# A hybrid decoder step on one core: the MLPs' down-projections by Strassen's scheme

## The chip, the cores and the metric

The program runs on one core of a Trainium2 chip. The metric is the device time of one execution in microseconds. The engines are TensorE (PE in the profile, its weight loads PEld), VectorE (DVE), ScalarE (ACT), GpSimd (POOL) and SyncE (SP), which only issues DMAs. They run side by side and wait for each other by semaphores.

## The reference

One inference step of a decoder with two trunk layers, for a prompt of 1024 tokens and 64 sample tokens, which share all weights: 1088 token columns. Layer 0 mixes by sparse and windowed attention, layer 1 by a gated linear recurrence. Each is followed by the MLP that the change is about:

```python
D_MODEL = 1024
D_FF = 4 * D_MODEL
def sq_relu_mlp(xn, w1, w2):
    h = jax.nn.relu(jnp.einsum('btd,df->btf', xn, w1))
    return jnp.einsum('btf,fd->btd', h * h, w2)
```

All is float32. `xn` is the RMS-normed x, and the result is added to x.

## The kernel before

**Layout.** Activations lie transposed: a tile has 128 features on the partitions and the 1088 columns in three chunks of 364, 364 and 360 (padded to 1092). `d.x` has the 8 tiles of x, `d.gh` and `d.gl` the high and low part of x times its gain. Every float32 product is made of three TensorE products of rounded values (fp32r): high x high, low weight x high, high weight x low (`Dense.product`, L2254 to 2269). So weights and activations are split: the high part is a rounded copy, the low part the difference.

**Weights** come in units of 128 x 1024 (512 KB), one per up tile (8 contraction tiles for one hidden tile) or, in the down-projection, one for two output tiles with four contraction tiles each. SP loads them into one of two slots of `unit_raw` (L2238 to 2241), DVE rounds (`split_high`, L2243 to 2246), POOL subtracts (`split_low`, L2248 to 2251). Both are done for unit u+2 while PE works on u+1, once u is free.

**MLP** (`stage_mlp`, from L2515). The 32 hidden tiles are worked in 8 blocks of `NF` = 4. `up(b)` makes 4 hidden tiles of 72 matmuls each. For each, ACT takes it from PSUM with a relu (L2617), DVE multiplies by the norm's reciprocal root (L2667), ACT squares into the rounded high part (L2619), DVE squares in float32 (L2672), POOL subtracts for the low part (L2593). `down(b)` makes a partial sum of 8 output tiles from these 4, 36 matmuls each, and DVE adds each to x (L2680). The first pair of output tiles takes the fourth hidden tile last (L2652 and on). Two PSUM tiles of three banks (`d_ps`) alternate in the up and the down part; `d_ps_sums` has the two banks between them, for sums of squares. The blocks 0 to 6 are a loop with register values in the waits, the last is written out.

**Around it.** At the end of the first MLP's last block, each finished tile of x is split for the next stage (`part_high` on ACT L2284, `part_low` on DVE L2289), squared (ACT, L2296), and POOL adds up the squares (`sum_up`, L2305). A stage begins with `opening`: its first two products and the matmuls that sum the squares over the partitions. The order of all this is that of the program text, engine by engine.

## Time and profile before

| | |
|---|---|
| median of 3 runs | 2729.66 us (2729.09 to 2733.43) |
| span of the profiled execution | 2722.7 us, 7.0 us less than the median |
| PE busy | 2632.0 us, 97% |
| DVE busy | 1141.8 us, 42% |
| POOL busy | 957.9 us, 35% |
| ACT busy | 781.5 us, 29% |
| attention and projections, until PE's chain of L2263 begins | 784 us |
| first MLP with its opening | 784 to 1617 us, about |
| recurrent stage | 1617 to 1945 us, about |
| second MLP | 1945 to 2719 us, about |

The page has the profiled execution's span and no other time of it; what lies around the span is taken as the 7.0 us to the median. A busy PE is not PE at its peak: the ends of matmuls are modelled and overlap, so the pace of the matmuls is read from their starts. A group's mean is the time of one instruction from start to end. L2263 is the line of nearly all dense matmuls, L2250 and L2246 those of all weight splits, so groups are told apart by the tiles' names.

### The profile page before, as it was taken

To read this page: it belongs to the slowest core of one execution; us is meant where nothing else is said; L and a number is where in the kernel's file an instruction comes from. 1 tells how busy PE (TensorE), PEld (TensorE's weight loads), DVE (VectorE), ACT (ScalarE), POOL (GpSimd) and SP (SyncE) were. 2 spreads that over 40 slices of the span, in tenths; PEclk is the share of its full clock that TensorE was granted. 3 is DMA by queue.
4 is the path that set the end of the run, shared out by engine and by line. 5 is a ranking of instruction groups with operands and counts; after the bars stand their busy time and mean duration, and the time that the engine had idled before them with its cause. 6 is when DMAs were issued, how large, how long until landed. Compare 5 with 4: busy or idle time off the path is not lost.

```text
span 2722.7 us, 39752 instructions
## 1 busy us (share of the span) xinstructions
PE 2632.0 (97%) x15960; PEld 2445.2 (90%) x15960; DVE 1141.8 (42%) x1978; ACT 781.5 (29%) x1400; POOL 957.9 (35%) x470
## 2 busy tenths in 40 slices
PE   7999999989889999999999999999999999999999
PEld 6667787857579999999999999988999999999999
DVE  5369875446555222222222266563532222222222
ACT  5357883866422001001001133452201001100100
POOL 4114440037245234234234362334334234333332
PEclk9999999989889999999999999999999999999999
DMA  4412223642641111111111111232111111111112
GB/s 145 135 26 80 84 89 105 205 113 76 193 178 50 44 46 40 45 46 46 39 46 44 41 54 57 96 130 101 41 47 41 44 46 39 46 45 39 46 43 85
DMA packets 109197, 198.65 MB, mean 73 GB/s; under 512 B 22710, under 2 KB 62774, under 8 KB 108806
## 3 DMA queue, kind: packets, MB, share of 16 engines
q1 hardware_dynamic: 104602, 191.85, 22.3%
q10 hardware_dynamic: 4480, 5.27, 0.6%
q8 instruction: 72, 1.18, 0.2%
q14 instruction: 43, 0.34, 0.0%
HBM read 170.97 MB, written 47.17 MB: 80 GB/s over the span
## 4 chain that ended last, share of the span: by engine, by line
PE 65%; issue 3%; POOL 2%; ACT 1%; DVE 1%; DMA 0%; POOLq 0%; DVEq 0%; ACTq 0%
PE d_ps L2263 63%; POOL m_hidden_low L2593 2%; PE d_ps L2886 1%; POOL unit_low L2250 1%; ACT m_relu L2617 1%; PE d_ps L2278 1%; DVE unit_high L2246 0%; PE d_ps_sums L2321 0%; POOL r_conv_in L2799 0%; DMA mixed_low<-mixed_t 0%; DVE mixed_low L2463 0%; POOL r_input_gate L2793 0%; POOLq L2539 0%; DVE xg_low L3014 0%; DVE x_t L2680 0%
## 5 line engine op out<-in xcount | busy, mean ns | idle before, releaser
L2250 POOL TENSOR_TENSOR unit_low<-unit_raw,unit_high 128x1024 fp32r<-128x1024 f32 x160 | 454.2, 2839 | 1192.0 <-DVE unit_high L2246 1191.3
L2263 PE MATMUL d_ps<-xg_high,unit_high 128*128 128x364 f32 (+1 forms) x2112 | 472.5, 332 | 6.9 <-DVE xg_low L3014 4.3
L2263 PE MATMUL d_ps<-xg_low,unit_high 128*128 128x364 f32 (+1 forms) x2112 | 465.1, 328 | 0.0
L2263 PE MATMUL d_ps<-xg_high,unit_low 128*128 128x364 f32 (+1 forms) x2112 | 465.0, 328 | 0.0
L2617 ACT ACTIVATE m_relu<-d_ps 128x1092 f32<-128x1092 f32 x64 | 69.2, 1082 | 1177.8 <-PE d_ps L2263 1177.8
L2680 DVE TENSOR_TENSOR x_t<-x_t,d_ps 128x1092 f32<-128x1092 f32 x128 | 165.3, 1292 | 520.1 <-PE d_ps L2263 520.1
L2263 PEld LDWEIGHTS d_ps<-xg_high,unit_high 128*128 128x128 f32 x2112 | 366.7, 189 | 11.8 <-DVE xg_low L3014 4.6
L2263 PEld LDWEIGHTS d_ps<-xg_high,unit_low 128*128 128x128 f32 x2112 | 367.2, 189 | 0.0
L2263 PEld LDWEIGHTS d_ps<-xg_low,unit_high 128*128 128x128 f32 x2112 | 365.7, 189 | 0.0
L2263 PE MATMUL d_ps<-m_hidden_high,unit_high 128*128 128x364 f32 (+1 forms) x1536 | 340.6, 330 | 3.8 <-POOL m_hidden_low L2593 3.8
L2263 PE MATMUL d_ps<-m_hidden_high,unit_low 128*128 128x364 f32 (+1 forms) x1536 | 338.5, 328 | 0.0
L2263 PE MATMUL d_ps<-m_hidden_low,unit_high 128*128 128x364 f32 (+1 forms) x1536 | 337.7, 328 | 0.0
L2667 DVE TENSOR_TENSOR m_relu<-m_relu,rstd_all 128x1092 f32<-128x1092 f32 x64 | 86.4, 1350 | 562.2 <-ACT m_relu L2617 562.2
L2263 PEld LDWEIGHTS d_ps<-m_hidden_high,unit_high 128*128 128x128 f32 x1536 | 264.0, 188 | 11.8 <-POOL m_hidden_low L2593 8.6
L2263 PEld LDWEIGHTS d_ps<-m_hidden_high,unit_low 128*128 128x128 f32 x1536 | 265.8, 188 | 0.0
L2263 PEld LDWEIGHTS d_ps<-m_hidden_low,unit_high 128*128 128x128 f32 x1536 | 265.6, 188 | 0.0
L785 PE MATMUL proj_ps<-w_high,x_high 128*128 128x512 f32 (+2 forms) x520 | 202.8, 390 | 13.7 <-POOL w_low L608 12.7
L785 PE MATMUL proj_ps<-w_low,x_high 128*128 128x512 f32 (+2 forms) x520 | 198.8, 382 | 0.0
L785 PE MATMUL proj_ps<-w_high,x_low 128*128 128x512 f32 (+2 forms) x520 | 198.3, 381 | 0.0
L2593 POOL TENSOR_TENSOR m_hidden_low<-m_square,m_hidden_high 128x1092 fp32r<-128x1092 f32 x64 | 163.4, 2554 | 6.4 <-DVE m_square L2672 6.4
L785 PEld LDWEIGHTS proj_ps<-w_high,x_high 128*128 128x128 f32 x520 | 99.8, 192 | 47.3 <-POOL w_low L608 13.9
L2246 DVE CAST unit_high<-unit_raw 128x1024 fp32r<-128x1024 f32 x158 | 111.8, 707 | 63.2 <-PE d_ps L2263 59.8
(370 smaller groups left out, 3090.0 us busy)
## 6 DMA issues: line engine op xcount, KB each, us to landing
unit_raw<-w_units SPq DMA_DIRECT2D x160, 512.0 KB, 3.6
unit_raw<-w_in SPq DMA_DIRECT2D x48, 256.0 KB, 2.9
proj_rows<-rows SPq DMA_DIRECT2D x32, 256.0 KB, 2.0
s_win<-win_cache SPq DMA_DIRECT2D x2, 3968.0 KB
proj_rows<-rows SPq DMA_DIRECT2D x36, 128.0 KB, 1.8
sw_rows<-proj_rows SPq DMA_DIRECT2D x12, 384.0 KB, 4.8
select_work<-xt SPq DMA_DIRECT2D x8, 546.0 KB, 4.1
x_t<-xt SPq DMA_DIRECT2D x4, 1092.0 KB, 13.6
```

The lines of the kernel that those rows point to most:

```text
L785: last = nc.tensor.matmul(ps[p % 3][:, 0:w], x[:, k, c:c + P], y[gi % 2][:, k, 0:w], start=(n == 0), stop=(n == len(passes) - 1))
L2246: self.nc.vector.tensor_copy(self.wh[slot][:, :], self.raw[:, slot, :]).then_inc(self.w_high, 1)
L2250: self.nc.gpsimd.tensor_tensor(self.wl[slot][:, :], self.raw[:, slot, :], self.wh[slot][:, :].bitcast(F32), ALU.subtract).then_inc(self.w_ ...
L2263: last = self.nc.tensor.matmul(ps[:, c, 0:USED[c]], w[wslot][:, wk], v[:, k, c, 0:USED[c]], start=(k == 0 and n == 0), stop=(k == nk - 1 a ...
L2278: last = self.nc.tensor.matmul(ps[:, c, 0:USED[c]], w[wslot][:, wk], v[:, k, c, 0:USED[c]], start=(k == 0 and n == 0), stop=(k == nk - 1 a ...
L2593: nc.gpsimd.tensor_tensor(hl[:, i, :, :], v[:, i % 2, :, :], hh[:, i, :, :].bitcast(F32), ALU.subtract).then_inc(h_low, 1)
L2617: nc.scalar.activation(r[:, i % 2, :, :], ps[slot][:, :, 0:CH], ACT.Relu).then_inc(d.taken[slot], 1)
L2667: nc.vector.tensor_tensor(r[:, i % 2, :, :], r[:, i % 2, :, :], d.rstd[:, :, :], ALU.mult).then_inc(relu_scaled, 1)
L2680: nc.vector.tensor_tensor(d.x[:, n, :, :], d.x[:, n, :, :], ps[s][:, :, 0:CH], ALU.add).then_inc(d.taken[s], 1)
L2886: last = nc.tensor.matmul(ps[use % 2][:, c, 0:CC], gw[:, n % 2, x, :], cv[:, n % 2, c, :], start=True, stop=True)
```

## The change

Both down-projections are computed by Strassen's scheme in Winograd's form. Take a pair of output tiles, two pairs of hidden tiles and the two halves of the columns (544 each): that is a 2 x 2 matrix of weights (each entry 256 deep) times a 2 x 2 matrix of hidden values, 8 half-size products. The scheme forms four sums of weights (`weigh`, DVE, 256 columns) and four sums of hidden values (`combine`, DVE, 544 columns), takes seven products (`part`), and adds them up in seven steps (`add`, DVE). Products 0 to 3 start four quarters of PSUM, products 4 to 6 go on in quarters 0, 2 and 3. What is common to several outputs gathers over all blocks in `shared_part` (`y2`) and is given out in the last block (`share`). Each product is 2 contraction tiles x 3 kinds x 2 chunks of 272 columns = 12 matmuls, so a block has 4 x 84 = 336 matmuls of 272 columns in its down-projection in place of 288 of 364, 364 and 360.

With it:
- The high parts of the hidden values are now ACT's copies of seven matrices of 544 columns per pair and contraction tile (`hidden_high`), the low parts POOL's (`hidden_low`); DVE takes the up product from PSUM with relu and reciprocal root in one (`spread_hidden`), ACT squares in place.
- A down unit is split in four parts, high by ACT (`high_of_parts`), low by POOL (`low_of_parts`), in place in the one pair of slots: the first half once product 3 of the pair before is done, the second once all seven are.
- Block b now makes the hidden tiles 4b+2 to 4b+5; the last block has two up tiles, and the pair made of them is used at once.
- A stage's opening waits for all adds of the MLP before it, since PSUM is shared.

```diff
+            def hidden_low(pair, q, s):
+                i = SPLIT_ORDER[s]
+                pool.wait_ge(h_high, NPROD * pair + s + 1)
+                nc.gpsimd.tensor_tensor(hl[:, i, q, :], SOURCES[i], hh[:, i, q, :].bitcast(F32), ALU.subtract).then_inc(h_low, 1)
...
+                for m in range(PAIRS):
+                    low_of_parts(PAIRS * b + m, m % 2, (2, 3) if last and m == 0 else range(4))
+                    if last and y is None:
+                        for o in (2 * m, 2 * m + 1):
+                            d.sum_up(pool, [v[:, i, :].rearrange("p (c n) -> p c n", c=NCH) for i in range(2)], o, seen)
+                if not last or y is None:
+                    for k in range(2):
+                        d.split_low(pool, W0 + NF * b + (6 if not last else 4) + k, k)
...
+            def high_of_parts(n, slot, which):
+                for x in which:
+                    act.wait_ge(wsums_made, 4 * n + (2, 3, 4, 4)[x])
+                    src, wide = weight_parts(d.raw[:, slot, :], wsum, x)
+                    nc.scalar.activation(part_slots(d.high, x), src, ACT.Copy).then_inc(part_high, 1)
...
+                for m in range(1, PAIRS):
+                    act.wait_ge(part_made, PART_MADE_0 + NPROD * (n + m - 1) + 4)
+                    high_of_parts(n + m, m % 2, (0, 1))
+                    act.wait_ge(part_made, PART_MADE_0 + NPROD * (n + m))
+                    high_of_parts(n + m, m % 2, (2, 3))
+                    if last and y is None:
+                        next_rows(m - 1)
...
+            def next_rows(m):
+                for o in (2 * m, 2 * m + 1):
+                    act.wait_ge(added, ADDED_0 + NPROD * (PAIRS * LAST + m) + 6 + o % 2)
+                    d.part_high(act, o, layer + 1)
+                    d.square(act, [v[:, i, :].rearrange("p (c n) -> p c n", c=NCH) for i in range(2)], o, seen)
...
+            def part(i, qs):
+                out = d.quarter[BLOCK_OF_PRODUCT[i]]
+                for q in qs:
+                    c0 = 2 * P * (i % 4) + P * q
+                    for x, (w, h) in enumerate(((d.high, hh), (d.low, hh), (d.high, hl))):
+                        for c in range(2):
+                            last = nc.tensor.matmul(out[:, c, :], w[:, i // 4, c0:c0 + P], h[:, i, q, HC * c:HC * (c + 1)],
+                                                    start=(i < 4 and q == 0 and x == 0),
+                                                    stop=(q == 1 and x == 2), skip_group_check=(i >= 4))
+                if qs[-1] == 1:
+                    last.then_inc(part_made, 1)
+
+            def ready(n, i):
+                pe.wait_ge(part_low, PART_LOW_0 + 4 * n + (1, 2, 1, 2, 3, 4, 3)[i])
+                pe.wait_ge(added, ADDED_0 + NPROD * n + (-2, -5, -1, 0, 1, 3, 4)[i])
...
+                        for i in range(4):
+                            if i == 2:
+                                pe.wait_ge(d.taken[1], R0 // 2 + pairs)
+                            ready(n, i)
+                            part(i, (0,))
+                        for i in range(4):
+                            pe.wait_ge(h_low, 2 * NPROD * b + NPROD + SPLIT_ORDER.index(i) + 1)
+                            part(i, (1,))
...
+            def spread_hidden(pair, t, first=False):
+                dve.wait_ge(d.made, R0 + 2 * pair + t + 1)
...
+                nc.vector.scalar_tensor_tensor(out=v[:, t, :].rearrange("p (c n) -> p c n", c=NCH), in0=d.ps[t][:, :, 0:CH], scalar=0.0,
+                                               in1=d.rstd[:, :, :], op0=ALU.max, op1=ALU.mult).then_inc(d.taken[t], 1)
...
+                for m in range(PAIRS):
+                    ahead = (n + m + 1, (m + 1) % 2, load_of(b, k0 + m + 1)) if m < PAIRS - 1 else None
+                    add(n + m, m, 0)
+                    if ahead:
+                        weigh(*ahead, 0)
+                    add(n + m, m, 1)
+                    if last:
+                        share(m)
...
+                    if not last and m == 1:
                         for x in range(2):
...
+                            combine(2 * b + 2, x)
+                    add(n + m, m, 4)
+                    add(n + m, m, 5)
```

**Order, POOL, last block of the first MLP, before.** `unit_low` is the low part of a whole unit, `square_sum` the running sum of the squares of x.

```order
L2250 TENSOR_TENSOR unit_low<-unit_raw,unit_high 128x1024
L2305 TENSOR_TENSOR square_sum<-square_sum,m_square 128x1092 x2
L2250 TENSOR_TENSOR unit_low<-unit_raw,unit_high 128x1024
L2305 TENSOR_TENSOR square_sum<-square_sum,m_square 128x1092 x2
L2250 TENSOR_TENSOR unit_low<-unit_raw,unit_high 128x1024
L2305 TENSOR_TENSOR square_sum<-square_sum,m_square 128x1092 x2
```

The same place after the change. The parts of 2 x 256 and 256 columns are the four lows of one pair of output tiles.

```order
L2655 TENSOR_TENSOR unit_low<-unit_raw,unit_high 128x2x256
L2655 TENSOR_TENSOR unit_low<-m_weight_sums,unit_high 128x2x256
L2655 TENSOR_TENSOR unit_low<-unit_raw,unit_high 128x2x256
L2655 TENSOR_TENSOR unit_low<-m_weight_sums,unit_high 128x256
L2325 TENSOR_TENSOR square_sum<-square_sum,m_hidden 128x1092 x2
L2270 TENSOR_TENSOR unit_low<-unit_raw,unit_high 128x1024 x2
```

Before, the low behind a pair of sums is that of a unit which PE takes one unit later; now all four lows of a pair stand behind the two sums of the pair before, and both units of the next opening behind the last two sums.

**Order, ACT, at the same place, after.** `unit_high` are the high parts of a pair of output tiles, `xg_high` and `m_hidden` the high part and the square of a row tile of x.

```order
L2713 ACTIVATE unit_high<-unit_raw 128x2x256
L2713 ACTIVATE unit_high<-m_weight_sums 128x256
L2304 ACTIVATE xg_high<-x_t,params 128x1092
L2316 ACTIVATE m_hidden<-x_t 128x1092
L2304 ACTIVATE xg_high<-x_t,params 128x1092
L2316 ACTIVATE m_hidden<-x_t 128x1092
```

The squares of a pair's two row tiles stand behind all high parts of the next pair; before, ACT had nothing but rows here.

**Order, DVE, second pair of output tiles in a middle block, after.** The adds read `d_ps`, the others are sums of weights and of hidden values; `square_sum` serves as their buffer.

```order
L2884 TENSOR_TENSOR x_t<-x_t,d_ps 128x544
L2873 REGISTER_ALU
L2874 REGISTER_ALU
L2875 TENSOR_TENSOR m_weight_sums<-unit_raw,m_weight_sums 128x256
L2842 REGISTER_ALU
L2844 REGISTER_ALU
L2845 TENSOR_TENSOR square_sum<-m_hidden 128x544
L2847 REGISTER_ALU
L2848 REGISTER_ALU
L2849 TENSOR_TENSOR m_hidden<-m_hidden 128x544
L2881 REGISTER_ALU
L2884 TENSOR_TENSOR x_t<-x_t,d_ps 128x544
```

Before, DVE had two adds of 128x1092 and one `unit_high` of 128x1024 (L2246) for a pair; now the fourth and the fifth add of a pair have a weight sum and two hidden sums between them.

## Rows read from the trace of the kernel before

**Rows 1.** Chain of waits, middle blocks of the first MLP: start us, us, what
```profile
1080.75 1.09 ACT m_relu L2617
...
1089.83 87.16 PE d_ps L2263 x522
1177.09 1.09 ACT m_relu L2617
```

**Rows 2.** TensorE in order of time at a down-projection's start: start us, us, instructions
```profile
992.08 0.66 PE L2263 MATMUL d_ps<-m_hidden_high,unit_low 128*128 128x364 f32 x3
...
992.58 0.66 PE L2263 MATMUL d_ps<-m_hidden_low,unit_high 128*128 128x364 f32 x3
...
993.49 0.77 PE L2263 MATMUL d_ps<-m_hidden_high,unit_high 128*128 128x364 f32 x3 [0.25 <-POOL m_hidden_low L2593]
```

**Rows 3.** The page's costliest groups: operation, shapes, count | busy us, mean ns | idle before
```profile
L2250 POOL TENSOR_TENSOR unit_low<-unit_raw,unit_high 128x1024 fp32r<-128x1024 f32 x160 | 454.2, 2839 | 1192.0 <-DVE unit_high L2246 1191.3
...
L2680 DVE TENSOR_TENSOR x_t<-x_t,d_ps 128x1092 f32<-128x1092 f32 x128 | 165.3, 1292 | 520.1 <-PE d_ps L2263 520.1
...
L2263 PE MATMUL d_ps<-m_hidden_high,unit_low 128*128 128x364 f32 (+1 forms) x1536 | 338.5, 328 | 0.0
...
L2593 POOL TENSOR_TENSOR m_hidden_low<-m_square,m_hidden_high 128x1092 fp32r<-128x1092 f32 x64 | 163.4, 2554 | 6.4 <-DVE m_square L2672 6.4
```

**Rows 4.** TensorE in order of time, matmuls of 256 columns, first and 26th
```profile
443.07 0.28 PE L785 MATMUL proj_ps<-w_low,x_high 128*128 128x256 f32 x1
...
446.05 0.28 PE L785 MATMUL proj_ps<-w_high,x_low 128*128 128x256 f32 x1
```

**Rows 5.** DVE's groups, shapes kept apart
```profile
L2672 DVE TENSOR_TENSOR m_square<-m_relu 128x1092 f32<-128x1092 f32 x64 | 82.5, 1288 | 0.1
...
L2116 DVE TENSOR_TENSOR ss_merge_shared<-select_work,ss_merge_shares 128x256 f32<-128x256 f32 x15 | 6.0, 453 | 0.0
...
L2956 DVE TENSOR_TENSOR r_conv_in<-d_ps,rstd_all 128x364 f32<-128x364 f32 x8 | 4.2, 524 | 0.0
```

**Rows 6.** ACT's groups, shapes kept apart
```profile
L2619 ACT ACTIVATE m_hidden_high<-m_relu 128x1092 fp32r<-128x1092 f32 x64 | 71.7, 1120 | 93.6 <-DVE m_relu L2667 93.6
...
L2284 ACT ACTIVATE xg_high<-x_t,params 128x1092 fp32r<-128x1092 f32 x24 | 28.6, 1206 | 78.2 <-DVE x_t L2507 47.2 <-DVE x_t L2680 30.4 <-PE d_ps L2263 0.6
...
L741 ACT ACTIVATE rows_sq<-rows 128x512 f32<-128x512 f32 x36 | 22.8, 632 | 3.6 <-ACT rows L721 0.4
```

**Rows 7.** POOL's groups, shapes kept apart
```profile
L608 POOL TENSOR_TENSOR w_low<-unit_raw,w_high 128x512 fp32r<-128x512 f32 x48 | 64.5, 1350 | 99.8 <-DVE w_high L928 99.8
...
L2305 POOL TENSOR_TENSOR square_sum<-square_sum,r_decay 128x1092 f32<-128x1092 f32 x3 | 7.2, 2409 | 0.0
...
L608 POOL TENSOR_TENSOR w_low<-unit_raw,w_high 128x256 fp32r<-128x256 f32 x8 | 6.7, 856 | 13.4 <-DVE w_high L928 13.4
```

**Rows 8.** In order of time, DVE and POOL at once, in two places
```profile
987.34 1.29 DVE L2672 TENSOR_TENSOR m_square<-m_relu 128x1092 f32<-128x1092 f32 x1
987.50 3.39 POOL L2250 TENSOR_TENSOR unit_low<-unit_raw,unit_high 128x1024 fp32r<-128x1024 f32 x1 [6.05 <-DVE unit_high L2246]
...
1612.83 3.46 POOL L2250 TENSOR_TENSOR unit_low<-unit_raw,unit_high 128x1024 fp32r<-128x1024 f32 x1 [2.25 <-DVE unit_high L2246]
1613.93 3.50 DVE L2289 SCALAR_TENSOR_TENSOR xg_low<-x_t,params,xg_high 128x1092 fp32r<-128x1092 f32 x1
```

**Rows 9.** TensorE in order of time behind two idle stretches
```profile
1836.65 3.32 PE L2886 MATMUL d_ps<-r_conv,own_a 128*128 128x371 f32 x6 [3.09 <-DVE square_sum L2979]
...
1852.23 1.28 PE L2263 MATMUL d_ps<-xg_high,unit_high 128*128 128x364 f32 x3 [4.29 <-DVE xg_low L3014]
...
1857.83 0.71 PE L2263 MATMUL d_ps<-xg_high,unit_high 128*128 128x364 f32 x3
```

**Rows 10.** Two stretches: us, each engine's busy us (count), granted clock, DMA share, GB/s
```profile
732.30:739.80 7.50, 6.96 (x138) 3.81 (x141) 4.79 (x23) 2.90 (x13) 2.91 (x4) 1.00 0.40 107
1855.00:1858.00 3.00, 3.00 (x12) 3.00 (x11) 2.97 (x3) 0.00 (x0) 0.00 (x0) 0.51 0.63 275
```

More of the change, by code:

```diff
@@ L2160 @@
 NBLK = FF // (NF * P)
-BLK_U, BLK_R = 2 * NF, NF + KD
+BLK_U = 2 * NF
 U_OUT = 0
@@ L2357, with stage_out_projection @@
 FIRST_KS = 4
-def stage_out_projection(nc, a, d, ident, mixed, own, oth, otl):
+def stage_out_projection(nc, a, d, ident, mixed, own, oth, otl, used):
     with ExitStack() as ctx:
@@ L2384, in stage_out_projection @@
         OWN = 16 * own.LOADS
+        freed = released(nc, used)
         @block.sync
@@ L2395, in _ @@
             for u in range(4, KD + 2):
-                d.load(sp, u, u % 2)
+                d.load(sp, u, u % 2, u)
         @block.gpsimd
         def _(pool):
+            for first, count in runs_of(freed):
+                nc.gpsimd.sem_clear(range(first, first + count))
             nc.gpsimd.memset(d.ones[:, :], 1.0).then_inc(d.ready, 1)
@@ L2558, in _, with run, unit_at, load_of @@
+        def run(eng, body):
+            with eng.Fori(0, LAST) as b:
+                body(b, False)
+            body(LAST, True)
+        def unit_at(b, k):
+            return U0 + 2 + BLK_U * b + k
+        def load_of(b, k):
+            return U0 // 2 + 1 + BLK_U // 2 * b + k // 2
+        def tile_at(b, k):
+            return NF * b + 2 + k
+        def down_at(b, last):
+            return 2 if last else NF
         @block.sync
         def _(sp):
-            def up(b):
-                for i in range(NF):
-                    u, slot = up_at(b, i)[:2]
-                    d.load(sp, u + 2, slot)
@@ L2565, in down, with load, body @@
-            def down(b):
-                for m in range(NF):
-                    u, slot = down_at(b, m)[:2]
-                    if not isinstance(u, int) or u + 2 < U_END:
-                        d.load(sp, u + 2, slot)
-            run(sp, up, down)
+            def load(u, slot):
+                if isinstance(u, int) and u >= U_END:
+                    return
+                d.load_unit(sp, u, slot)
+            def body(b, last):
+                k0 = down_at(b, last)
+                for k in range(k0):
+                    sp.wait_ge(d.w_low, W0 + tile_at(b, k) + 1)
+                    load(unit_at(b, k + 2), k % 2)
+                for m in range(PAIRS):
+                    sp.wait_ge(part_low, PART_LOW_0 + 4 * (PAIRS * b + m) + 4)
+                    load(unit_at(b, k0 + m + 2), m % 2)
@@ L2596, in down @@
[L2596 to L2605 removed]
+            nc.gpsimd.sem_inc(part_made, PART_MADE_0)
@@ L2607, in _ @@
+            pool.wait_ge(d.made, R0 + 1)
+            nc.gpsimd.memset(y2[:, :, :], 0.0).then_inc(cleared, 1)
+            for k in range(2):
+                d.split_low(pool, W0 + k + 2, k)
+            run(pool, body)
         @block.scalar
@@ L2621, in down, with square_hidden @@
-            def down(b):
-                if isinstance(b, int) and y is None:
-                    for n in range(KD):
-                        _, _, _, _, slot, used = down_at(b, n // 2)
-                        act.wait_ge(d.taken[(slot + n) % 2], used + (slot + n % 2) // 2 + 1)
-                        d.part_high(act, n, layer + 1)
-                        d.square(act, [v[:, 0, :, :], v[:, 1, :, :]], n, seen)
-            run(act, up, down)
+            def square_hidden(tile, t):
+                act.wait_ge(d.taken[t], R0 // 2 + tile + 1)
+                nc.scalar.activation(v[:, t, :], v[:, t, :], ACT.Square).then_inc(squared, 1)
@@ new lines, in next_rows @@
+            def next_rows(m):
[3 more added lines that the diff above has]
+                    d.square(act, [v[:, i, :].rearrange("p (c n) -> p c n", c=NCH) for i in range(2)], o, seen)
+            for t in range(2):
+                square_hidden(0, t)
+            act.wait_ge(d.made, R0 + 2)
+            unit_high(W0 + 3, 1, U0 // 2 + 1)
+            run(act, body)
@@ L2656, in _, with up @@
-            run(pe, up, down)
+            d.opening(pe, W0, R0, nth)
+            def up(b, k):
+                t = k % 2
+                pe.wait_ge(d.w_low, W0 + tile_at(b, k) + 1)
+                pe.wait_ge(d.taken[t], R0 // 2 + 2 * b + 1 + k // 2)
+                pe.wait_ge(added, ADDED_0 + NPROD * (PAIRS * b - 1) + (5 if t == 0 else NPROD))
+                d.product(pe, d.ps[t], t, 0, KD, d.gh, d.gl)
+            def part(i, qs):
[9 more added lines that the diff above has]
+                    last.then_inc(part_made, 1)
@@ new lines, in _, with weight_parts @@
+            for t in range(2):
+                spread_hidden(0, t, True)
+            dve.wait_ge(cleared, 1)
+            for x in range(2):
+                combine(0, x, True)
+            run(dve, body)
+        return added, ADDED_0 + NPROD * PAIRS * NBLK
+def weight_parts(raw, wsum, x):
+    if x < 2:
+        src = raw[:, 0:4 * P] if x == 0 else wsum[:, 0:2, :].rearrange("p a n -> p (a n)")
+    else:
+        src = raw[:, 4 * P:8 * P] if x == 2 else wsum[:, 2, :]
+    return (src.rearrange("p (a n) -> p a n", a=2), 2) if x < 3 else (src, 1)
```

389 lines of the change are left out of this document (264 added, 125 removed).

## The prediction

> **What bounds the kernel now.** I read the chain of waits first. In both MLPs it is TensorE, interrupted once per block of four hidden tiles: 87.16 us of L2263, then ACT, DVE and POOL in turn, and again [rows 1]. One block lasts 1177.09 - 1080.75 = 96.34 us and holds 576 matmuls, 288 up and 288 down. The view in order of time shows what the interruption costs: three matmuls start every 0.50 us, but between 992.58 and 993.49 there are 0.91 us, because the down-projection waits for the fourth tile's low part from POOL; with the slow restart it is about 0.6 us [rows 2]. So a matmul of 362.7 columns on average costs (96.34 - 0.6) / 576 = 166.2 ns, and nothing else in the MLPs matters. The costliest groups show how much room the other engines have: POOL's hidden lows, L2593, are 163.4 us in the whole run, its unit lows, L2250, 454.2, DVE's adds, L2680, 165.3 [rows 3].
>
> The profiled span is 2722.7 us; the times shown have a median of 2729.66, so 7.0 us lie around the span. All differences below are put on the span and carried to that median.
>
> **Matmuls.** Down-projections now: 3 x 1536 = 4608 matmuls (one of the three groups, which differ by 1%, stands in [rows 3]); 4608 x 166.2 ns = 765.8 us. After: 16 blocks x 4 pairs of output tiles x 7 products x 12 matmuls = 5376, of 272 columns. No row has 272 columns. Between 443.07 and 446.05, 25 matmuls of 256 columns start, 119.2 ns each [rows 4], also with a weight load for each; between that and 166.2 ns at 362.7 the line gives 126 ns at 272. 5376 x 126 = 677.4 us: **-88.3 us**. Bounds: 119.2 (-125) and 133 ns (-51). I take the line, close to the 256 row. A fixed part of some 7 ns per matmul eats 3 us of the 91.5 us for which the columns alone stand. The Trainium skill (TensorE: Matmul & The Clock Gate, Back-to-back issue gap) has columns / 2.4 plus 2.5 ns, so 153.6 ns before and 115.8 after, and the sum would be -85.3 us; the trace has more time at both sizes.
>
> The old wait goes with the old order: 16 x 0.6 = **-9.6**. In the middle blocks hidden pair 2b+1 is made two up tiles before it is used, 24 us (2 x 72 x 166.2 ns), and its seven highs and lows need 7 x 0.66 on ACT and 7 x 1.36 on POOL (544 columns; between 0.63 for 512 and 1.12 for 1092 on ACT, 1.35 and 2.55 on POOL [rows 3, 6, 7]): hidden. PSUM is now released by DVE, behind the reciprocals of an opening, and no longer by ACT ahead of them; DVE's 1.3 us bound what the first up tile can wait for that (0 to 1.3, twice), I take 0.4: **+0.8**.
>
> **DVE and POOL in the middle blocks.** A pair of output tiles lasts 84 x 126 = 10.6 us on PE. DVE has seven adds (0.71 each, between 0.52 for 364 and 1.29 for 1092 columns) and four weight sums (0.45, as L2116): 6.8 us [rows 3, 5]. POOL has lows of 512, 512, 512 and 256 columns, 1.35 x 3 + 0.86 = 4.9 us [rows 7]. Both fit. But they block each other: L2672, with both inputs in SBUF, beside L2250 makes the latter 3.39 us for 1024 columns, where L2305 has 2.41 for 1092 [rows 7], and L2289, begun 1.1 us into an L2250, lasts 3.50, where L2672 has 1.29 for as many columns [rows 5, 8]. The Trainium skill (SBUF - State Buffer, Who interferes with whom) says it as a lock held for a whole instruction by whichever started first, when the DVE instruction has two SBUF inputs. The trace agrees with its 3.39 and 3.50 us; it speaks against this change, since weight sums, hidden sums and lows are all of that kind.
> It shows at the step from the second pair to the third, where two hidden sums (0.73 each) stand ahead of the fifth add, and the first product of the next pair needs that add. From the end of the fourth product (6.05 us into the pair) DVE does 0.71 + 0.45 + 1.46 + 0.71 and handovers of 0.3: 9.7 of 10.6 us, 0.9 left. POOL's two lows of 1.3 fall in the same stretch. Once in the way they cost 0.4, twice 1.7; which, hangs on whether ACT's high (0.63) or DVE's add (0.71) ends first. I take 1.2 x 14 blocks = **+16.8** (0 to 24).
>
> **The last block of each MLP** has two up tiles, and hidden pair 15 is used at once. From the end of the second: DVE 1.3, ACT square 1.12, DVE sum 0.73, ACT high 0.66, two lows 2.7, handovers 0.4: 6.9 us. PE has four half products and one more, 3.8 us: wait 3.1. Then product 5 needs the low of the third weight part, which on POOL stands behind all seven hidden lows, and the last of these behind DVE's fourth sum: two lows 2.7, sum 0.73, high 0.66, low 1.36, part low 1.3 = 6.8 after 6.9, less what PE does meanwhile (2.3): 4.5, and with DVE's L2892/L2893 (0.73 + 1.29) in POOL's way up to 7.4. I take 6.2. Together 9.3 x 2 = **+18.6** (15 to 21).
>
> **The last block of the first MLP** is the worst place. POOL adds up the squares of rows 2m and 2m+1 before it makes any low of pair m+1 (the order shows it), and these squares are ACT's last work behind the highs of pair m+1, which wait for pair m's last product. So PE ends pair m, and then: highs 0.63 + 0.42, the rows' high and square (L2304, L2316) twice, (1.21 + 1.12) x 2 = 4.7, POOL's sum 2.4 to 2.6, the first low 1.3, handovers 0.3 to 0.6: 9.7, 10.1 and 10.1 us of idle PE, **+29.9** [rows 3, 6, 7]. Before, the next unit's low stood ahead of these sums, one unit early; that cover is gone. The recurrent stage's opening hangs on the same: unit high 1.06, 4.7, sum 2.5, POOL behind one xg_low of DVE 1.3, unit low 2.3, handovers 0.5: **+12.4** (10 to 14). The second MLP has no squares.
>
> **Clock.** After 4.29 us of idle PE, from 1852.23 on, the granted clock was half, 0.51 between 1855 and 1858 [rows 9, 10]. From 1852.23 to 1857.83 PE starts 18 matmuls in 5.60 us, where 18 x 166.2 ns are 3.0: 2.6 us lost. After the 3.09 us at 1836.65 six matmuls of 371 columns take 3.32 us, 0.55 each, and I take less, 2.0. Six new gaps are longer (three between pairs, the opening, one per last block): 6 x 2.3 = **+13.8** (9 to 20). A slow stretch ahead of the second wait of a last block disappears in it.
>
> The end is shorter: the last add 0.71 instead of 1.29, **-0.6**.
>
> Sum: -88.3 - 9.6 + 0.8 + 16.8 + 18.6 + 29.9 + 12.4 + 13.8 - 0.6 = -6.2. On 2729.7 that is 2723.5, so **2724 us**. Of 98.5 us won, 92.3 are spent again, 9.3 + 29.9 + 12.4 + 5 x 2.3 = 63 of them in the first MLP's last block.
>
> **Rivals.**
> *The engines stay out of each other's way.* DVE wins the port: 0.4 us per middle block, 7.5 per last block, gaps of 9 us with 2 us of clock. -6.2 - 11.2 - 3.6 - 4 = -25: 2705. For it: POOL and DVE are busy for 35% and 42% of the span now, by the table. Against: their starts come from the same product's end.
> *DVE becomes the bound in the middle blocks (slower).* Four weight sums per pair, each behind a low of 1.3, are 6.8 + 5.2 = 12.0 against 10.6 us of PE. If half of this comes true, each of the 14 blocks waits 3 us instead of 1.2: +25, 2749. It decides for slower than before once a middle block waits over 1.7 us. For it: nearly every DVE step also has two or three register steps ahead of it. Against: lows fill only 4.9 of 10.6 us.
> *PE's queue or the weight load sets the pace.* A product is 24 instructions and two or three register steps in 1.51 us, 56 ns each; the row of 256 columns shows 59.6 ns and no less. Were that the floor, a product would take 1.61: +0.1 x 392 = +38, 2762. Against: 138 matmuls and 141 loads in 7.5 us at 732.3, 27 ns each, though of smaller tiles [rows 10].
> *The order does not bite* (the squares come early enough, so the gaps of the first MLP's last block are not there): 2724 - 42 - 9 = 2673. The order speaks plainly against it.
>
> **Numbers.** Forecast 0.55, first rival 0.2, second 0.14, third 0.06, fourth 0.05. The forecast's own range is 2712 to 2736. A measurement of this kernel tells 0.2%, 5.5 us, from no change, so faster means below 2724.2: half of the forecast's weight lies there. Faster 0.27 + 0.2 + 0.05 = 0.52, same 0.24, slower 0.04 + 0.14 + 0.06 = 0.24. Range 2700 to 2746.
>
> **What would show it.** Sets of two matmuls of 272 columns 0.25 us apart; middle blocks of 48 + 42.3 + 1.2 = 91.5 us in the chain; in the last block of the first MLP three gaps of about 10 us on PE that end with a POOL low of 512 columns, behind a POOL sum, and one of 12 ahead of the opening; half clock behind each. If the gaps are there but the blocks last 90.5 us, the first rival is right; if PE's sets are 0.27 apart without waits, the third. A total below 2700 means that I misread the order.

## The result and the profile after

| | before | after |
|---|---|---|
| median | 2729.38 us (2727.72 to 2733.43, 4 runs) | 2714.87 us (2708.61 to 2716.01, 4 runs) |
| span of the profiled execution | 2722.7 us | 2714.2 us (its own time 2716.01) |

The ratio is 0.9948 [0.9935, 0.9961]: 14.5 us faster, 9 us below the forecast of 2724 and inside its range. Around the span of after lie 1.8 us, not the 7.0 assumed for before. In all executions that are listed with both, span and time differ by 1.7 to 1.9 us, so the profiled execution of before took about 2724.6 us, some 5 us less than its median. That is why the two profiled executions differ by 8.5 us only and the medians by 14.5.

The page after, engines first (busy us, share, instructions), then groups (operation, shapes, count | busy us, mean ns | idle before):

```profile
PE 2561.0 (94%) x16728; PEld 2370.2 (87%) x16728; DVE 1505.1 (55%) x2510; ACT 1043.2 (38%) x1876; POOL 1201.4 (44%) x824
...
L2785 PE MATMUL d_ps<-m_hidden_high,unit_high 128*128 128x272 f32 x1792 | 379.3, 294 | 53.0 <-POOL unit_low L2655 35.9
...
L2655 POOL TENSOR_TENSOR unit_low<-unit_raw,unit_high 128x512 fp32r<-128x512 f32 x128 | 177.6, 1387 | 392.0 <-ACT unit_high L2713 392.0
L2884 DVE TENSOR_TENSOR x_t<-x_t,d_ps 128x544 f32<-128x544 f32 x320 | 227.3, 718 | 151.6 <-PE d_ps L2785 151.2
L2648 POOL TENSOR_TENSOR m_hidden_low<-m_hidden,m_hidden_high 128x544 fp32r<-128x544 f32 x192 | 272.0, 1439 | 77.5 <-ACT m_hidden_high L2702 77.5
```

The adds and lows have the sizes that were put between the neighbours of [rows 3, 5, 7] (forecast 0.71, 1.35 and 1.36 us). PE has less to do than before and is still the chain's main engine, but 35.9 us of its idle time are now POOL's weight lows.

One middle block in the chain of waits (start us, us, what), where [rows 1] had ACT's relu and 87.16 us of one piece:

```profile
942.88 0.72 DVE x_t L2884
943.60 0.04 issue
943.64 21.37 PE d_ps L2785 x168
965.01 47.84 PE d_ps L2283 x288
1012.86 21.12 PE d_ps L2785 x168
1033.98 0.04 issue
1034.01 0.72 DVE x_t L2884
```

A block lasts 1034.01 - 942.88 = 91.13 us (before 96.34), and 168 matmuls of 272 columns take 21.12 us, 125.7 ns each. It is cut once, ahead of the third pair of output tiles. In order of time, on PE, DVE and POOL:

```profile
942.42 0.41 PE L2785 MATMUL d_ps<-m_hidden_low,unit_high 128*128 128x272 f32 x2
943.64 0.52 PE L2785 MATMUL d_ps<-m_hidden_high,unit_high 128*128 128x272 f32 x2 [0.81 <-DVE x_t L2884]
```

```profile
939.41 1.82 DVE L2845 TENSOR_TENSOR square_sum<-m_hidden 128x544 f32<-128x544 f32 x1
941.26 1.70 DVE L2849 TENSOR_TENSOR m_hidden<-m_hidden 128x544 f32<-128x544 f32 x1
942.88 1.97 DVE L2884 TENSOR_TENSOR x_t<-x_t,d_ps 128x544 f32<-128x544 f32 x3
```

```profile
939.15 1.49 POOL L2655 TENSOR_TENSOR unit_low<-unit_raw,unit_high 128x512 fp32r<-128x512 f32 x1 [4.06 <-ACT unit_high L2713]
940.60 1.77 POOL L2655 TENSOR_TENSOR unit_low<-m_weight_sums,unit_high 128x512 fp32r<-128x512 f32 x1
```

DVE's two hidden sums last 1.82 and 1.70 us, not 0.73, each beside a low of POOL's; the fifth add (the first of L2884 at 942.88) comes late and PE loses 1.0 us (1.10 from start to start, where 0.126 is usual). It is so in all 14 middle blocks.

The last block of the first MLP, the chain from the end of its second pair of output tiles:

```profile
1577.67 0.94 ACT unit_high L2713 x2
1578.61 1.09 ACT xg_high L2304
1579.70 1.01 ACT m_hidden L2316
...
1580.78 2.50 POOL square_sum L2325
...
1583.42 2.48 POOL square_sum L2325
1585.90 1.23 POOL unit_low L2655
1587.13 0.04 issue
1587.17 13.60 PE d_ps L2785 x84
```

This is the forecast's chain, step for step; PE's waits from start to start are 9.36, 9.83, 9.83 us, and 12.11 ahead of the opening. For the opening the chain of waits has 10.62 us of "issue" and names nobody. POOL in order of time shows what it waits for:

```profile
1625.96 6.16 POOL L2325 TENSOR_TENSOR square_sum<-square_sum,m_hidden 128x1092 f32<-128x1092 f32 x2 [12.55 <-ACT m_hidden L2316]
1632.08 4.67 POOL L2270 TENSOR_TENSOR unit_low<-unit_raw,unit_high 128x1024 fp32r<-128x1024 f32 x2
```

The first of the two unit lows ends about where PE goes on, at 1634.52. Behind the waits the granted clock is at its lower level, 1.2 of 2.4 GHz, and 84 matmuls take 13.60 us where two pairs of a middle block have 21.12 for 168. Two of the stretches (us, each engine's busy us, clock, DMA):

```profile
1580.00:1593.00 13.00, 5.83 (x25) 5.83 (x26) 1.06 (x2) 2.80 (x3) 9.36 (x6) 0.50 0.12 33
1604.00:1613.50 9.50, 3.19 (x14) 3.20 (x15) 0.07 (x1) 1.93 (x2) 9.27 (x6) 0.50 0.00 0
```

By stage, from PE's starts in order of time (first matmul of the out-projection; first of the four that sum the squares, in each opening; PE's end), profiled executions, us:

| kernel (median) | ahead of the out-projection | to the first sums | first MLP | recurrent | second MLP |
|---|---|---|---|---|---|
| before (2729.4) | 762.2 | 87.9 | 772.6 | 334.6 | 760.7 |
| after (2714.9) | 771.3 | 87.6 | 789.2 | 331.4 | 729.5 |
| e1 lows first (2684.4) | 769.9 | 88.9 | 756.2 | 334.9 | 729.6 |
| e2 hidden sums late (2698.4) | 766.5 | 88.9 | 783.3 | 331.5 | 720.9 |
| e3 short lows (2697.6) | 766.4 | 88.1 | 782.4 | 331.4 | 720.9 |
| e4 before, small scratch (2729.7) | 765.3 | 88.7 | 772.8 | 335.0 | 761.0 |
| e5 parts early (2718.8) | 769.1 | 88.4 | 790.2 | 334.6 | 729.4 |
| e6 three orders (2667.3) | 766.0 | 88.6 | 750.8 | 333.0 | 721.9 |
| e7 short sums (2682.9) | 766.9 | 89.0 | 753.3 | 334.6 | 729.6 |
| e8 busy waits (2709.9) | 767.2 | 87.9 | 784.5 | 335.0 | 728.6 |
| e9 share behind 4th add (2671.5) | 766.2 | 88.7 | 751.9 | 335.1 | 723.9 |
| e10 share behind 7th add (2662.1) | 766.9 | 88.0 | 747.5 | 335.0 | 718.7 |

So the change makes the second MLP 31.3 us shorter and the first 16.6 longer. The first column is the same work in all kernels: it moves by 9 us over these executions and blurs a comparison of two spans. (The two kernels without the change have its two lowest values, 762.2 and 765.3; that the change costs a little there is not excluded.)

### The profile page after: what moved, and what is told of

The parts are those of the page before. It is cut to its first block, busy times and chain, and to the rows that moved or that the text cites. A ratio compares the mean times of both kernels' runs of the same rounds, so it can differ in the third digit from the quotient of the medians.

```text
span 2714.2 us, 44747 instructions
## 1 busy us (share of the span) xinstructions
PE 2561.0 (94%) x16728; PEld 2370.2 (87%) x16728; DVE 1505.1 (55%) x2510; ACT 1043.2 (38%) x1876; POOL 1201.4 (44%) x824
## 4 chain that ended last, share of the span: by engine, by line
PE 65%; DVE 3%; issue 1%; POOL 1%; ACT 1%; DMA 0%; DVEq 0%; ACTq 0%; POOLq 0%
PE d_ps L2283 39%; PE d_ps L2785 24%; PE d_ps L3164 1%; PE d_ps L2298 1%; DVE x_t L2884 1%; POOL square_sum L2325 0%; DVE square_sum L2845 0%; DVE rstd_all L2370 0%; POOL m_hidden_low L2648 0%; DVE xg_low L3292 0%; POOL unit_low L2655 0%; DVE m_hidden L2837 0%; PE d_ps L2343 0%; DVE unit_high L2266 0%; POOL unit_low L2270 0%
## 5 line engine op out<-in xcount | busy, mean ns | idle before, releaser
L2283 PE MATMUL d_ps<-xg_high,unit_high 128*128 128x364 f32 (+1 forms) x2112 | 472.5, 332 | 18.8 <-issue 11.8
L2785 PE MATMUL d_ps<-m_hidden_high,unit_high 128*128 128x272 f32 x1792 | 379.3, 294 | 53.0 <-POOL unit_low L2655 35.9
L2270 POOL TENSOR_TENSOR unit_low<-unit_raw,unit_high 128x1024 fp32r<-128x1024 f32 x96 | 231.2, 2409 | 405.3 <-DVE unit_high L2266 237.6
L2785 PE MATMUL d_ps<-m_hidden_high,unit_low 128*128 128x272 f32 x1792 | 374.2, 290 | 0.0
L2785 PE MATMUL d_ps<-m_hidden_low,unit_high 128*128 128x272 f32 x1792 | 373.6, 290 | 0.0
L2655 POOL TENSOR_TENSOR unit_low<-unit_raw,unit_high 128x512 fp32r<-128x512 f32 x128 | 177.6, 1387 | 392.0 <-ACT unit_high L2713 392.0
L2884 DVE TENSOR_TENSOR x_t<-x_t,d_ps 128x544 f32<-128x544 f32 x320 | 227.3, 718 | 151.6 <-PE d_ps L2785 151.2
L2648 POOL TENSOR_TENSOR m_hidden_low<-m_hidden,m_hidden_high 128x544 fp32r<-128x544 f32 x192 | 272.0, 1439 | 77.5 <-ACT m_hidden_high L2702 77.5
L2713 ACT ACTIVATE unit_high<-unit_raw 128x512 fp32r<-128x512 f32 x128 | 81.0, 633 | 517.8 <-PE d_ps L2785 381.4
L2702 ACT ACTIVATE m_hidden_high<-m_hidden 128x544 fp32r<-128x544 f32 x192 | 118.9, 651 | 224.6 <-DVE m_hidden L2857 129.3
L2837 DVE SCALAR_TENSOR_TENSOR m_hidden<-d_ps,rstd_all 128x1092 f32<-128x1092 f32 x64 | 82.5, 1291 | 206.7 <-PE d_ps L2283 204.8
```

The lines of the kernel that those rows point to most:

```text
L2270: self.nc.gpsimd.tensor_tensor(self.wl[slot][:, :], self.raw[:, slot, :], self.wh[slot][:, :].bitcast(F32), ALU.subtract).then_inc(self.w_ ...
L2283: last = self.nc.tensor.matmul(ps[:, c, 0:USED[c]], w[wslot][:, wk], v[:, k, c, 0:USED[c]], start=(k == 0 and n == 0), stop=(k == nk - 1 a ...
L2648: nc.gpsimd.tensor_tensor(hl[:, i, q, :], SOURCES[i], hh[:, i, q, :].bitcast(F32), ALU.subtract).then_inc(h_low, 1)
L2655: nc.gpsimd.tensor_tensor(out, src, top.bitcast(F32), ALU.subtract).then_inc(part_low, 1)
L2702: nc.scalar.activation(hh[:, i, q, :], SOURCES[i], ACT.Copy).then_inc(h_high, 1)
L2713: nc.scalar.activation(part_slots(d.high, x), src, ACT.Copy).then_inc(part_high, 1)
```

## The experiments

**Lows ahead of the sums of squares** (POOL, last block; result 2684.4 us (2680.3 to 2687.6), ratio to before 0.9827 [0.9804, 0.9850])

```diff
-                for m in range(PAIRS):
-                    low_of_parts(PAIRS * b + m, m % 2, (2, 3) if last and m == 0 else range(4))
+                low_of_parts(PAIRS * b, 0, (2, 3) if last else range(4))
+                for m in range(PAIRS):
+                    if m < PAIRS - 1:
+                        low_of_parts(PAIRS * b + m + 1, (m + 1) % 2, range(4))
+                    elif not last or y is None:
+                        for k in range(2):
+                            d.split_low(pool, W0 + NF * b + (6 if not last else 4) + k, k)
                     if last and y is None:
                         for o in (2 * m, 2 * m + 1):
                             d.sum_up(...)
```

> The changed kernel with one thing moved on POOL, in the last block only: the four lows of a pair of output tiles, and behind the last pair the two unit lows of the next opening, stand ahead of the sums of squares of the pair before. My theory: the order on POOL alone makes the four waits of 9.36, 9.83, 9.83 and 12.11 us; they go but for about 0.9 us ahead of the opening (the last add), 40 us, and with them four of the half-clock stretches, 9 us: 2715 - 49 = about 2666. Rival: ACT or DVE would be late anyhow (the highs wait for the same product), so that each wait only shrinks to some 4 us: 2715 - 25 = about 2690.

Measured: -30.5 us, the first MLP 33.0 shorter and now 16.4 below that of before. So mending the order gave 33 us, where 40 + 9 were put on it; the median, 2684.4, is nearer to the rival's 2690 than to the 2666 of the theory. The waits of 9 to 12 us are gone, waits of 1.3 to 3.7 us have come in their place, and they end with DVE's adds. Of 40 us there, DVE is busy for 38.7 (columns as above):

```profile
1557.00:1597.00 40.00, 30.39 (x223) 29.49 (x222) 38.70 (x36) 18.52 (x23) 28.43 (x16) 0.96 0.14 40
```

In order of time, DVE and POOL:

```profile
1588.37 0.71 DVE L2886 TENSOR_TENSOR m_shared_part<-m_shared_part,d_ps 128x544 f32<-128x544 f32 x1
...
1590.12 2.70 DVE L2894 TENSOR_TENSOR x_t<-x_t,m_shared_part 128x544 f32<-128x544 f32 x1
1592.74 3.60 DVE L2895 TENSOR_TENSOR x_t<-x_t,m_shared_part 128x1088 f32<-128x1088 f32 x1
```

```profile
1586.90 2.08 POOL L2655 TENSOR_TENSOR unit_low<-unit_raw,unit_high 128x512 fp32r<-128x512 f32 x1 [2.77 <-ACT unit_high L2715]
...
1589.64 5.54 POOL L2325 TENSOR_TENSOR square_sum<-square_sum,m_hidden 128x1092 f32<-128x1092 f32 x2
1595.15 3.43 POOL L2270 TENSOR_TENSOR unit_low<-unit_raw,unit_high 128x1024 fp32r<-128x1024 f32 x1
```

The instruction of 1088 columns takes 3.60 us beside POOL's sums and the low behind them, where the one in the chain of e5 below has 1.29; the add of one input from PSUM has its 0.71 beside a low. Two of DVE's groups in these 40 us, weight sums of 256 columns, and the same sum in e3, where POOL's lows are short:

```profile
L2867 DVE TENSOR_TENSOR m_weight_sums<-unit_raw 128x256 f32<-128x256 f32 x2 | 3.6, 1792 | 0.0
L2870 DVE TENSOR_TENSOR unit_raw<-unit_raw 128x256 f32<-128x256 f32 x2 | 3.1, 1553 | 0.1
...
940.61 0.42 DVE L2867 TENSOR_TENSOR m_weight_sums<-unit_raw 128x256 f32<-128x256 f32 x1
```

At the times that they have elsewhere (adds 0.71, row lows 1.27, shared part 0.72 and 1.29, weight sums 0.42) DVE's instructions there would take some 27 us, an estimate. So some 12 us or more of DVE's busy time there are stretch beside POOL. My theory has the cause of the old waits right, the rival (DVE late anyhow) the size of what is left.

**Hidden sums late** (DVE; 2698.4 us (2696.6 to 2699.1), 0.9881 [0.9861, 0.9901])

```diff
-                    if not last and m == 1:
-                        for x in range(2):
-                            combine(2 * b + 2, x)
                     add(n + m, m, 4)
...
                     add(n + m, m, 6)
+                    if not last and m == 1:
+                        for x in range(2):
+                            combine(2 * b + 2, x)
```

> The changed kernel with the two hidden sums of the second pair of output tiles moved behind that pair's last add, so that they no longer stand ahead of the fifth. My theory: the 1.10 us from start to start at the step from the second to the third pair (0.13 elsewhere) go in all 14 middle blocks, 14 x 1.0 = 14 us: about 2701. Rival: DVE is late by its whole load, and the wait turns up at a later product: about 2715.

Measured: -16.4 us; no wait is left in the middle blocks (no two starts over 0.2 us apart), and the two MLPs are 5.9 and 8.6 us shorter.

**Short lows** (POOL makes the weight lows of the second to fourth pair for 32 of 256 columns in middle blocks; the rest of them is left out; 2697.6 us (2691.9 to 2704.6), 0.9882 [0.9854, 0.9911])

```diff
+                    if few:
+                        out, src, top = (t[..., 0:32] for t in (out, src, top))
```

> The changed kernel, with POOL's lows of the second to fourth pair of output tiles made for 32 of each 256 columns in the middle blocks (that part of the low weights is left out); DVE's and ACT's orders as they are. If the 1.0 us at the step to the third pair is the price of POOL's lows standing in DVE's way, it goes here too: about 2702. If it is DVE's queue alone (two hidden sums ahead of the fifth add), it stays: about 2715.

Measured: -17.3 us, the same waits gone, with DVE's order as it was. The two hidden sums, DVE in order of time:

```profile
935.00 0.85 DVE L2847 TENSOR_TENSOR square_sum<-m_hidden 128x544 f32<-128x544 f32 x1
935.88 0.73 DVE L2851 TENSOR_TENSOR m_hidden<-m_hidden 128x544 f32<-128x544 f32 x1
```

1.82 and 1.70 have become 0.85 and 0.73. The wait needs both: POOL's lows beside the hidden sums, and these ahead of the fifth add. "DVE's queue alone" is refuted.

**Before with the small scratch** (2729.7 us (2728.4 to 2735.2), 1.0003 [0.9993, 1.0013])

```diff
-    nc = bacc.Bacc("TRN2", target_bir_lowering=False, num_devices=1)
+    nc = bacc.Bacc("TRN2", target_bir_lowering=False, num_devices=1, dynamic_dma_scratch_size=1024)
```

> The kernel before, with only the smaller scratch of 1024 for dynamic DMAs that the change also brings. In the profiled execution of after, the part ahead of the first MLP lasts 9 us longer, from the sample stage at 731 us on. If the scratch is why: 2729 + 9 = about 2738. If it is the chance of one execution, or the clock: about 2729.

The scratch does nothing; the 9 us are the spread of one stage from execution to execution (first column of the table).

**Third and fourth part early** (last block of both MLPs; 2718.8 us (2715.4 to 2722.3, 3 runs), 0.9956 [0.9940, 0.9973])

```diff
                     for s in range(2, NPROD):
                         hidden_low(2 * b + 1, 1, s)
+                        if s in (4, 5):
+                            low_of_parts(PAIRS * b, 0, (s - 2,))
```
and `high_of_parts(n, 0, (2, 3))` on ACT behind the fifth hidden high.

> The changed kernel; in the last block of both MLPs ACT and POOL make the third and fourth part (high, low) of the first pair of output tiles between the hidden parts for products 4, 5 and 6, not behind all of them. My theory: the second wait of a last block (3.47 and 4.86 us from start to start) is POOL's order. Now product 4 waits for two lows from the end of the first wait on, 2.8 us against 2.3 us of PE, product 5 for two more, and these waits come to about 2 us in place of 3.3 and 4.7: 4 us less in all, about 2711. Rival: DVE's sums and adds are what is late, and the waits stay.

Refuted: the rival holds. In the second MLP product 4 now waits 1.6 us from start to start and product 5 another 4.2, 5.8 in all where product 4 alone had waited 4.9, and both waits end with an add of DVE's. The chain there:

```profile
2671.12 0.04 DVE x_t L2894
2671.16 1.69 issue
2672.86 1.29 DVE x_t L2895
2674.14 0.02 issue
2674.17 0.43 DVE unit_raw L2870
2674.59 0.64 DVE x_t L2886
```

Product 5 needs the third add, and the giving out of the shared part (L2894, L2895) stands ahead of it.

**All three orders** (2667.3 us (2666.2 to 2667.4), 0.9764 [0.9749, 0.9779])

The edits are the three above: those of lows ahead of the sums (e1), hidden sums late (e2) and parts early (e5).

> All three orders together: lows ahead of the sums of squares, hidden sums behind the second pair's last add, third and fourth part of the last block's first pair early. If the three are independent: 2684.4 (the first alone) - 14 (2698.4 against 2714.9 in the second alone would be 16) - 4 = about 2665. If DVE's load sets the last block of the first MLP once POOL's order is mended, the third gives nothing there: about 2669.

2667.3 lies between the two (2665 and 2669): e1's 30.5 and e2's 16.4 add up to 46.9, measured 47.6. So the two parts made early add nothing that can be told from noise, and the result does not decide between the two expectations.

**Short sums of squares** (e1; POOL adds six of the seven squares of the first MLP's last block over 32 of 364 columns, the rest is left out; 2682.9 us (2680.5 to 2691.1), 0.9833 [0.9815, 0.9850])

```diff
+        out, first, second = (t[:, :, 0:32] if seen == KD and n > 1 else t for t in (self.ssum[:, :, :], first, sq[n % 2]))
```

> The kernel with the lows ahead of the sums of squares (2684.4 us), and six of the seven sums of squares of the first MLP's last block made on POOL over 32 of each 364 columns (the rest of these sums is left out); DVE and ACT do all they did. In that block a pair of output tiles now takes 16 us where PE needs 10.6. If that is DVE and POOL shutting each other out: DVE's instructions with both inputs in SBUF (four weight sums 1.8, the shared part 2.0, two row lows 2.5 us) and POOL's (lows 4.9, sums 4.8) are 16.0 in a row, and without the sums 11.3, so that DVE's own 11.4 are the bound: three pairs x 4.6 = 14 us less, 2684 - 14 = about 2670. If DVE's own load with its waits is the bound, nothing changes: about 2684.

Mostly refuted: 1.5 us in the medians, which is within the noise, 2.9 in the stage, not 14. From the first add of the third pair to that of the fourth it is 12.2 us (1569.67 to 1581.89) where e1 has 15.8 (1572.57 to 1588.37), near the 11.3 that was expected; but the opening then waits 5.6 us for the last add, behind two row lows of DVE stretched to 3.4 and 3.2 us, and its clock falls (72 matmuls in 13.77 us, where 166.5 ns each make 12.0). DVE is busy for 35.7 of 37 us even so:

```profile
1554.00:1591.00 37.00, 31.81 (x248) 31.02 (x246) 35.71 (x39) 19.44 (x24) 22.32 (x16) 1.00 0.15 44
```

**Busy waits** (after, 72 matmuls of 240 columns into free columns of PSUM ahead of the second to fourth pair; 2709.9 us (2707.6 to 2711.6), 0.9920 [0.9906, 0.9934])

```diff
+                    if last and y is None and m:
+                        pe.wait_ge(added, ADDED_0 + NPROD * n - 5)
+                        for j in range(72):
+                            nc.tensor.matmul(banks_free[j % 2], hh[:, 0, 0, 0:P], hh[:, 1, 0, 0:240], start=True, stop=True)
```

> The changed kernel; in the first MLP's last block, ahead of the second, third and fourth pair of output tiles, PE does 72 extra matmuls of 240 columns into unused columns (about 8 us of the waits of 9.4 to 9.8). Nothing is left out. If the half clock behind these waits comes from the idle PE, it stays away, and the three stretches give back 2.4 + 3.0 + 1.9 us less what the extra matmuls push: 2715 - 7 = about 2708. If the clock falls for another reason: 2715 or a little more.

Measured: -5.0 us, the first MLP 4.7 shorter, by a kernel that does 216 matmuls more. Three stretches of 10 us there, all at the full clock:

```profile
1560.00:1570.00 10.00, 8.88 (x71) 8.82 (x71) 6.94 (x11) 1.27 (x2) 4.31 (x4) 1.00 0.19 54
1570.00:1580.00 10.00, 10.00 (x88) 9.87 (x87) 4.00 (x5) 5.15 (x6) 4.70 (x2) 1.00 0.00 0
1580.00:1590.00 10.00, 8.40 (x67) 8.34 (x67) 6.46 (x11) 1.27 (x2) 4.79 (x5) 1.00 0.19 55
```

The half clock behind the waits comes from the idle PE: with matmuls in them it stays away.

**Shared part behind the fourth add** (on e6; 2671.5 us (2671.2 to 2673.5), 0.9787 [0.9767, 0.9807]) and **behind the seventh** (2662.1 us (2660.3 to 2668.0), 0.9756 [0.9740, 0.9772]). The second, which the first differs from by the place:

```diff
-                    if last:
-                        share(m)
+                    if last and m == PAIRS - 1:
+                        share(m, 2)
...
                     add(n + m, m, 6)
+                    if last and m < PAIRS - 1:
+                        share(m, 7)
```
Those who read the finished rows wait for `spread` too.

> The kernel with all three orders (2667.3 us) and, in the last block of both MLPs, the giving out of the shared part (DVE, 1.8 and 1.3 us) moved from behind the second add of a pair to behind the fourth. With the third and fourth part early, product 5 of the first pair waited 4.2 us for the third add, which stood behind the shared part. My theory: that wait falls to about 1 us in both MLPs, 6 us less, and the other pairs of the first MLP gain nothing, since DVE is busy all the time there: about 2661. If POOL's parts are late by then anyway (product 4 or 6), half of it: about 2664. If the third add was not what it waited for: 2667.

Refuted, 4 us slower: product 5 waits 1.0 us, but the first product of the second pair now waits 3.0 us (product 0 needs the fifth add), and in the second MLP the next two pairs 1.9 each.

> The kernel with all three orders (2667.3 us); in the last block of both MLPs the shared part is given out behind the seventh add of a pair (first to third pair; the fourth as before), where PE needs nothing of DVE for 6 us. Behind the fourth add (2671.5 us) it stood ahead of the fifth, for which the next pair's first product waits. My theory: the wait of product 5 of the first pair falls from 4.2 to about 1 us in both MLPs, and no other comes in its place: 6 us less, about 2661; in the first MLP up to 5 more, since the third to fifth adds of each pair come earlier. If DVE's sum of work sets the first MLP's last block, only the second MLP gains: 2664. If the wait moves again: 2667 or more.

5.2 us faster than e6, where 6 were expected: 3.3 in the first MLP and 3.2 in the second, where behind the first wait of 3.1 us only one of 0.9 and one of 1.6 are left. In the first MLP the wait moved again: product 5 of the first pair no longer waits, but the third pair now waits 4.1 us and the opening 5.5. There ACT's row tiles wait for the shared part, the highs of the third pair stand behind them, and POOL begins a sum of squares ahead of their first low (ACT and POOL in order of time):

```profile
1549.14 0.61 ACT L2717 ACTIVATE unit_high<-unit_raw 128x512 fp32r<-128x512 f32 x1
...
1549.38 3.12 POOL L2325 TENSOR_TENSOR square_sum<-m_hidden 128x1092 f32<-128x1092 f32 x1 [5.71 <-ACT m_hidden L2316]
1552.46 2.32 POOL L2656 TENSOR_TENSOR unit_low<-unit_raw,unit_high 128x512 fp32r<-128x512 f32 x1
```

This version is 68.7 us (ratio 0.9756) below before and 52.8 below after.

## Why the prediction was right, and where it was off

The direction, the mechanism of each term and the order of sizes held. The gain itself did not: 14.5 us by the medians where some 6 were forecast. It is the small difference of two large sums (98.5 won, 92.3 spent), so misses of 2 to 5 us in several terms more than double it. That the total came within 9 us is in part luck: 15.7 us of misses on one side were offset by 3.9 on the other, and by some 3 us between the stages of two single executions and the medians. Dense stages of after less before: +16.6 - 3.1 - 31.3 = -17.8 us, forecast -6.2. Step by step:

- **Matmuls**, -88.3. 125.7 ns against 126. With before's waits at 0.41 us (0.57 from start to start less one matmul) a matmul there is 166.5 ns, so 4608 x 166.5 - 5376 x 125.7 = 767.2 - 675.8 = -91.4. Right. The "fixed part of some 7 ns" was summed wrongly: over the 768 matmuls more it is 5.4 us, not 3; the -88.3 does not use it. The Trainium skill (TensorE: Matmul & The Clock Gate, Back-to-back issue gap) has columns / 2.4 plus 2.5 ns for an isolated matmul, which gives an estimate of 115.8 ns. The trace has 12 ns above the columns' 113.3, in a stream where each matmul has its own weight load.
- **Old wait**, -9.6: 16 x 0.41 = -6.6. I had added a slow restart that the starts don't show.
- **Entry**, +0.8: 2 x 0.85 = +1.7.
- **Middle blocks**, +16.8: 14 x 0.97 = +13.6. That POOL's lows stretch the two hidden sums is shown by e3, their place in the order by e2. The Trainium skill (SBUF - State Buffer, Who interferes with whom) has a shared port pair, locked by one engine at a time, on which a DVE instruction with two SBUF inputs meets a POOL instruction that reads SBUF. By it the first sum, begun at 939.41 beside a low that ends at 940.64, would last 1.23 + 0.73 = 1.96 us, an estimate; the trace has 1.82, and 0.85 in e3.
- **Last block's first pair**, +18.6: 3.0 + 3.3 in the first MLP, 3.0 + 4.7 in the second, +14. The first wait was exact (3.1); the second, taken at 6.2, was over-sized. (What the prediction there calls product 5 is product 4 in the count from 0.) The sum gave 4.5, and 6.5 with the two instructions of the shared part in the way, not 7.4; the 4.7 measured in the second MLP is close to the plain sum. In the first MLP it is shorter since PE runs at half clock ahead of it (0.56 there, 1.00 at the same place in the second MLP); from the end of the first wait to that of the second it is 7.1 us in both, so the half clock costs nothing there, as the prediction said. Whether the clock falls behind this wait is not fixed by the code there: in e2, where the last block is unchanged, it falls in the second MLP and not in the first. What the pair hangs on was told only in part: e5 shows that the third add, behind the shared part, is as late as POOL's lows.
- **Three waits and the opening**, +29.9 and +12.4: 28.6 and 12.0. Right, and by the steps named. e1 shows the cause, POOL's order: with it mended these four waits are gone.
- **Clock**, +13.8: what is left of the first MLP, 16.6 + 45.7 + 3.3 - 0.9 - 6.8 - 6.3 - 28.6 - 12.0 = 11 for five stretches, and in the same way 2.4 in the second MLP. Right, as a remainder; two of the stretches can be read directly, 84 matmuls in 12.96 and 13.60 us where 10.56 are usual, 2.4 and 3.0 us. e8 gets about 5 of it back by keeping PE busy.
- **Recurrent stage**, 0: -3.1, not foreseen. The wait of 4.3 us ahead of the stage's own out-projection, with half clock behind it [rows 9, 10] is, after, three shorter ones with the full clock behind them:

```profile
1870.33 0.77 PE L2283 MATMUL d_ps<-xg_high,unit_high 128*128 128x364 f32 x3 [1.40 <-DVE xg_low L3292]
...
1874.59 0.77 PE L2283 MATMUL d_ps<-xg_high,unit_high 128*128 128x364 f32 x3 [0.98 <-DVE xg_low L3292]
...
1877.02 0.76 PE L2283 MATMUL d_ps<-xg_high,unit_high 128*128 128x364 f32 x3 [0.67 <-DVE xg_low L3292]
```

In the table the stage takes 331.4 us with after, e2 and e3, 333 with e6, and 335 with all others. The change gave the stage's code a later opening and new numbers of its weight units and little else, and the others but before and e4 have these too. What sends it one way or the other stays open.

The 11.6 us between -6.2 and -17.8 are many small ones, which add up to 11.8: first pair 4.6, middle blocks 3.2, recurrent stage 3.1, matmuls 3.1, waits at the pairs and the opening 1.7, less 3.9 for the old wait and the entry. None is over 5 us. By the medians the kernels are 14.5 apart and not 17.8; the 3 us between lie in the spread of the executions. The 7.0 us around the span were an assumption that no row bore out.

By its total alone the result does not tell the forecast (2724) from the first rival (2705): 2714.9 lies halfway. Nor does the length of a middle block, 91.1 between 91.5 and 90.5. The rows decide: DVE's hidden sums last 1.82 and 1.70 us and the wait is 0.97, not 0.4, in all 14 blocks, so the engines do get in each other's way. The third rival is refuted by the pace, 125.7 ns a matmul (its +38 also counts only 392 of 448 products). The fourth is refuted by the four waits.

"DVE becomes the bound" is wrong for the middle blocks (DVE waits there) but half right for a place that I had not looked at: the first MLP's last block, once POOL's order is mended. I should have made DVE's sum for that block as well: seven adds, four weight sums, shared part and two row lows, 5.0 + 1.8 + 2.0 + 2.5 = 11.3 us per 10.6 us of PE, before any stretching. But a pair took 15.8 us in e1, so most of what is over 10.6 is stretch and waiting for each other. No run makes DVE's own work less there, so how the rest is shared between the two is not shown.

## What to carry to other kernels

Cutting an eighth of PE's work in one part costs the other engines more instructions; what it yields is decided by the order of each queue at the steps where their results are needed. Here 58 us of waits and clock in one block of sixteen (6.3 + 28.6 + 12.0 + 11) ate most of the gain, and four moves of a few lines each (lows ahead of sums that nobody waits for soon, hidden sums and the shared part behind the last add, two parts earlier) brought 52.8 us together, more than three times what the scheme brought by itself. The first two brought nearly all of it (46.9 by their runs alone). Two parts earlier brought nothing by itself (e5 2718.8, after 2714.9), and whether the shared part's move needs it was not tried. When a wait is mended, ask which semaphore of the same product is next: in e5 and e9 the wait only moved to the next add.

## What was not expected of the hardware

- Two DVE instructions with both inputs in SBUF, of 544 columns, last 0.73 to 0.85 us where POOL's lows are cut short and 1.70 to 1.82 beside full lows; one of 1088 columns 3.60 beside POOL's sums, 1.29 in e5; one of 256 columns 1.79 and 1.55 on average in e1's last block, 0.42 in e3. An add with one input in PSUM keeps its 0.71 us beside a low of POOL's.
- Extra matmuls made a kernel faster: 216 of them in waits of PE kept the granted clock at 1.00 and gave back 5.0 us.
- Behind one and the same wait of 3.1 us the clock fell in one MLP and not in the other (0.56 and 1.00 in after), and the other way round in e2.
- The stage ahead of the out-projection, the same work in twelve profiled executions, takes 762.2 to 771.3 us.
